# An attention and product-key expert layer: V's gathers ahead of U's, the second keys' one-hot rows of tile 1 on ScalarE, and a different split of the slots at the end

## The reference

```python
q = (h @ w_query).reshape(B, S, PEER_HEADS, 2, PEER_HALF)
s = jnp.einsum('bshcd,hckd->bshck', q, sub_keys)
top_s, top_i = lax.top_k(s, PEER_TOPK)                 # 16 of 128 first keys, 16 of 128 second keys
cand = top_s[..., 0, :, None] + top_s[..., 1, None, :]
best_s, best_i = lax.top_k(cand, PEER_TOPK)            # 16 pairs of them
eid = i1 * N_KEYS + i2                                 # expert = 128 * first key + second key
g = jax.nn.softmax(best_s, axis=-1)
a = jax.nn.gelu(jnp.einsum('td,thkd->thk', hx, expert_u[e]))
out = jnp.einsum('thk,thkd->td', gw * a, expert_v[e])  # 8 heads x 16 experts per token
```

## Time and profile before

| what | value |
|---|---|
| runs, median (lowest to highest) | 1754.23 us (1752.3 to 1754.84) |
| profiled execution: time, span | 1752.67 us, 1750.9 us |
| mean granted TensorE clock | 0.933 of full speed |
| PE, DVE, POOL, ACT busy | 85%, 78%, 55%, 22% of the span |
| DMA, mean | 351 GB/s |
| gathers of U and of V | 256 and 256 |

### The profile page before, as it was taken

How to read it: one execution, slowest core, us unless ns; L and a number is a source line. 1 busy time by engine, 2 the same in 40 slices (tenths; PEclk the granted TensorE clock), 3 DMA queues, 4 the chain that set the end, 5 groups by cost and what they waited for, 6 DMA issues and landing times.

```text
span 1750.9 us, 16867 instructions
## 1 busy us (share of the span) xinstructions
PE 1487.4 (85%) x6164; PEld 931.8 (53%) x6164; DVE 1360.2 (78%) x1915; ACT 380.5 (22%) x822; POOL 967.4 (55%) x591
## 2 busy tenths in 40 slices
...
DMA  9876443466799999999999999999999999999994
GB/s 319 279 262 217 121 145 121 145 203 230 297 380 412 374 424 425 412 425 426 421 424 426 415 425 422 420 426 409 415 427 360 377 414 409 401 404 410 423 428 186
DMA packets 159379, 615.38 MB, mean 351 GB/s; under 512 B 20915, under 2 KB 74255, under 8 KB 96703
## 3 DMA queue, kind: packets, MB, share of 16 engines
q0 software_dynamic: 79232, 485.32, 67.6%
...
HBM read 683.42 MB, written 2.10 MB: 392 GB/s over the span
## 4 chain that ended last, share of the span: by engine, by line
PE 29%; POOL 19%; DMA 19%; DVE 18%; issue 12%; DVEq 2%; ACT 1%; SPq 0%; POOLq 0%; ACTq 0%
DMA v_slot<-in_expert_v_dram,eid 15%; PE psum_all L587 13%; POOL v_slot L542 11%; DVE u_slot L1764 9%; POOL u_slot L525 9%; PE psum_all L727 4%; DVE xh L1799 4%; PE psum_all L976 3%; DMA u_slot<-in_expert_u_dram,eid 2%; PE psum_all L752 2%; PE psum_all L708 1%; PE psum_all L614 1%; PE psum_all L612 1%; PE psum_all L938 1%; DMA wq_ring<-in_w_query_dram 0%
## 5 line engine op out<-in xcount | busy, mean ns | idle before, releaser
L976 PE MATMUL psum_all<-v_slot,diag 128*128 128x512 f32 x1152 | 557.2, 636 | 154.5 <-DMA v_slot<-in_expert_v_dram,eid 108.9
L1764 DVE SCALAR_TENSOR_TENSOR u_slot<-u_slot,xh 128x2048 f32<-128x2048 f32 x256 | 576.2, 2287 | 91.3 <-DMA u_slot<-in_expert_u_dram,eid 90.0
L525 POOL DMA_INDIRECT u_slot<-in_expert_u_dram,eid x256 | 441.7, 1726 | 302.7 <-DVE u_slot L1764 136.7
L542 POOL DMA_INDIRECT v_slot<-in_expert_v_dram,eid x224 | 424.6, 1895 | 94.5 <-issue 64.7
L976 PEld LDWEIGHTS psum_all<-v_slot,diag 128*128 128x128 f32 x1152 | 224.1, 202 | 464.1 <-issue 255.4
L1799 DVE SCALAR_TENSOR_TENSOR xh<-v_slot,gate,xh 128x2048 f32<-128x2048 f32 x112 | 263.4, 2352 | 53.9 <-DMA v_slot<-in_expert_v_dram,eid 46.3
L1382 DVE TENSOR_TENSOR w_lo<-w_ring,w_hi 128x512 fp32r<-128x512 f32 x240 | 156.6, 688 | 78.3 <-ACT w_hi L1012 75.1
L587 PE MATMUL psum_all<-act_hi,w_hi 128*128 128x256 f32 x640 | 185.2, 289 | 1.1 <-DVE w_lo L1382 1.0
L587 PE MATMUL psum_all<-act_hi,w_lo 128*128 128x256 f32 x640 | 181.1, 283 | 0.0
L587 PE MATMUL psum_all<-act_lo,w_hi 128*128 128x256 f32 x640 | 181.0, 283 | 0.0
L1012 ACT ACTIVATE w_hi<-w_ring 128x512 fp32r<-128x512 f32 x240 | 139.4, 622 | 42.7 <-PE psum_all L587 41.5
...
...
## 6 DMA issues: line engine op xcount, KB each, us to landing
...
u_slot<-in_expert_u_dram,eid POOLq DMA_INDIRECT x256, 19.2
v_slot<-in_expert_v_dram,eid POOLq DMA_INDIRECT x256, 18.2
```

The lines of the kernel that those rows point to most:

```text
L525: nc.gpsimd.indirect_dma_start(out=u_slot[m % RU][:, :], out_offset=None, in_=expert_u[0], in_offset=bass.IndirectOffsetOnAxis(ap=eid[:, n ...
L542: nc.gpsimd.indirect_dma_start(out=v_slot[m % RV][:, :], out_offset=None, in_=expert_v[0], in_offset=src, bounds_check=ROWS - 1, oob_is_er ...
L976: ins = nc.tensor.matmul(bank[(4 if n < PH else 0) + q][:, :], diag[:, n % 2, k, :], v_slot[m % RV][:, 512 * q:512 * q + 512], start=(m in ...
L1764: V.scalar_tensor_tensor(u_slot[m % RU][:, :], u_slot[m % RU][:, :], 1.0, xh[:, n // PH, :], ALU.mult, ALU.mult, accum_out=u_dot[:, n, k:k ...
```

## The change

In the gather order GpSimd issues 64 + (m + 1) * 8 / 7 of U's before V's m, so V's run closer behind, and 28 of U's, not 5, are left to be issued in one row before V's gather 144. The ring of dense pieces shrinks from 8 slots to 4 (`RD`) and the distance between the tiles from 3 to 2 (`LEAD`). The four other slots of U join V's ring, from V's gather 151 on (`LATE`), so that V has 11 slots in the last stage. All blocks of tile 1 are built by TensorE behind its last V pick; before they stood between the picks 132 to 143 and behind. For tile 1 ScalarE makes the 128-wide one-hot rows as relu(1 - |iota - key|), eight Abs of 128 columns and one Relu of 1024 per block (`key_rows`); VectorE makes them for tile 0 only. The blocks of tile 0 stand at slightly other places.

```diff
-RD = 8
+RD = 4
-LEAD = 3
+LEAD = 2
+LATE = V0_PICKS + TOPK + RV
+RING_V = list(range(RV, RV + RU - RD)) + [m % RV for m in range(V0_PICKS + TOPK, LATE)]
-HOT0_AT = {180 + 5 * b // 2: b for b in range(NG_T)}
+HOT0_AT = {178 + 2 * b: b for b in range(NG_T)}
...
+    v_slot += u_slot[RD:]
...
-            if m >= PE_PICKS + RV:
-                pool.wait_ge(S["v_dve"], m - RV - PE_PICKS + 1)
+            if LATE <= m < LATE + RU - RD:
+                pool.wait_ge(S["dots_done"], TOPK * NU - RU + v_place(m) - RV + RD + 1)
+            if m >= LATE + RU - RD:
+                pool.wait_ge(S["v_dve"], m - len(RING_V) - PE_PICKS + 1)
...
-            while sent < min(TOPK * NU, TOPK * AHEAD + (m + 1) * 13 // 10):
+            while sent < min(TOPK * NU, TOPK * AHEAD + (m + 1) * 8 // 7):
...
+            if t:
+                pe.wait_ge(S["key_ok"], b + 1)
...
-                pe.wait_ge(S["pick_ok"], 2)
-            if m == V0_PICKS - 2:
-                pick_transposes(1)
-            if m >= V0_PICKS + 4:
-                if m == V0_PICKS + 4:
-                    pe.wait_ge(S["part_ok"], 1)
-                dense_rows(1, m - V0_PICKS - 4)
...
-        for b in range(TOPK - 4, NG_T):
+        pe.wait_ge(S["part_ok"], 1)
+        pick_transposes(1)
+        for b in range(NG_T):
             dense_rows(1, b)
...
+        def key_rows(b):
+            g, n = NG_T + b, PICKS[1]
+            act.wait_ge(S["dense_mm"], g - 1)
+            for i in range(G_TOK):
+                nc.scalar.activation(hot2[0:n, g % 2, i, :], iota_key[0:n, :], ACT.Abs,
+                                     bias=pickT[0:n, 1, 1, G_TOK * b + i:G_TOK * b + i + 1])
+            act.drain()
+            nc.scalar.activation(hot2[0:n, g % 2, :, :], hot2[0:n, g % 2, :, :], ACT.Relu, bias=one_col[0:n, :], scale=-1.0
+                                 ).then_inc(S["key_ok"], 1)
...
+        unit(13)
+        picks_out(1)
+        key_rows(0)
         for b in range(NG_T):
+            if b + 1 < NG_T:
+                key_rows(b + 1)
             if b == 8:
+                expo_gate(14)
+                expo_gate(15)
                 gelu_unit(14)
             dense_out(1, b)
```

More of the change, by code:

```diff
@@ L48, with v_place, v_times @@
 IDS_AT.update({(n, 1): n + 1 for n in range(1, 9)})
-HOT0_AT = {180 + 5 * b // 2: b for b in range(NG_T)}
+HOT0_AT = {178 + 2 * b: b for b in range(NG_T)}
 HOT1_AT = {14 * TOPK + 5 + 3 * b // 2: b for b in range(NG_T)}
+def v_place(m):
+    return m % RV if m < LATE else RING_V[(m - LATE) % len(RING_V)]
+def v_times(m):
+    return sum(1 for i in range(m + 1) if v_place(i) == v_place(m))
 HTW = SEQ + 2
@@ L293, in build @@
     eps = at("eps", [P, 2], F32)
+    one_col = at("one_col", [P, 1], F32)
     warm = at("warm", [P, 1], F32)
@@ L323, in build @@
     s_v = [nc.alloc_semaphore(f"s_v{i}") for i in range(RV)]
+    s_v += [nc.alloc_semaphore(f"s_e{i}") for i in range(RU - RD)]
     s_d = [nc.alloc_semaphore(f"s_d{i}") for i in range(RD)]
@@ L464, in _ @@
         nc.gpsimd.memset(eps[:, 1:2], LN_EPS)
+        nc.gpsimd.memset(one_col[:, :], 1.0)
         nc.gpsimd.memset(cu[:, :, :], 0.0)
@@ L537, in gather_v @@
                 pool.wait_ge(S["v_used"], m - RV + 1)
[L538 to L539 removed]
+            if LATE <= m < LATE + RU - RD:
+                pool.wait_ge(S["dots_done"], TOPK * NU - RU + v_place(m) - RV + RD + 1)
+            if m >= LATE + RU - RD:
+                pool.wait_ge(S["v_dve"], m - len(RING_V) - PE_PICKS + 1)
             src = bass.IndirectOffsetOnAxis(ap=eid[:, n, k:k + 1], axis=0)
             if n < NU - 2:
[L542 to L546 removed]
+                nc.gpsimd.indirect_dma_start(out=v_slot[v_place(m)][:, :], out_offset=None, in_=expert_v[0], in_offset=src,
+                                             bounds_check=ROWS - 1, oob_is_err=False).then_inc(s_v[v_place(m)], 16)
+            else:
+                nc.gpsimd.indirect_dma_start(out=v_slot[v_place(m)][:, :], out_offset=None, in_=expert_v[0], in_offset=src
+                                             ).then_inc(s_v[v_place(m)], 16)
         for m in range(TOPK * AHEAD):
@@ L958, in _ @@
                 pick_transposes(0)
-            if m % 2 and 93 <= m < 93 + 2 * NG_T:
-                dense_rows(0, (m - 93) // 2)
+            if m % 2 and 97 <= m < 97 + 2 * NG_T:
+                dense_rows(0, (m - 97) // 2)
             if m == V0_PICKS:
@@ L1308, in picks_out @@
             n = PICKS[t]
-            nc.scalar.activation(pickT[0:n, t, :, :].rearrange("p a t -> p (a t)"), bank[2 + t][0:n, 0:3 * P], ACT.Copy
-                                 ).then_inc(S["pick_ok"], 1)
+            src = bank[(2, 6)[t]]
+            if t:
+                nc.scalar.activation(pickT[0:n, t, 1, :], src[0:n, P:2 * P], ACT.Copy, scale=-1.0)
+                nc.scalar.activation(pickT[0:n, t, 0, :], src[0:n, 0:P], ACT.Copy)
+                nc.scalar.activation(pickT[0:n, t, 2, :], src[0:n, 2 * P:3 * P], ACT.Copy).then_inc(S["pick_ok"], 1)
+                act.drain()
+            else:
+                nc.scalar.activation(pickT[0:n, t, :, :].rearrange("p a t -> p (a t)"), src[0:n, 0:3 * P], ACT.Copy
+                                     ).then_inc(S["pick_ok"], 1)
+        def key_rows(b):
[4 more added lines that the diff above has]
+                                     bias=pickT[0:n, 1, 1, G_TOK * b + i:G_TOK * b + i + 1])
+            act.drain()
+            nc.scalar.activation(hot2[0:n, g % 2, :, :], hot2[0:n, g % 2, :, :], ACT.Relu, bias=one_col[0:n, :], scale=-1.0
+                                 ).then_inc(S["key_ok"], 1)
         def dense_out(t, b):
@@ L1348, in _ @@
                 diagonals(7)
-            if b in (5, 11):
-                unit(11 + b // 11)
+            if b == 7:
+                unit(11)
             if b == 11:
                 diagonals(8)
+            if b == 15:
+                unit(12)
             dense_out(0, b)
-        unit(13)
-        picks_out(1)
         act.wait_ge(S["t0_part"], 1)
```

19 lines of the change are left out of this document (7 added, 12 removed).

## The result

| | before | changed |
|---|---|---|
| median (lowest to highest) | 1753.26 us (1750.02 to 1754.84, 4 runs) | 1786.4 us (1781.92 to 1792.76, 4 runs) |
| ratio to before | 1 | 1.0193, 95% interval 1.0165 to 1.022 |
| profiled span | 1750.9 us | 1786.5 us |
| mean granted clock of TensorE | 0.933 | 0.927 |

The change costs 33 us. Slower was the likeliest side of the prediction, but 1786 us lies 20 us above its number and 4 us outside its range.

The account below looks back on a forecast made before the run. DMA was taken as full to about 1700 us, with VectorE ending last and 29 us of dense-stage slack. Start 1408 + 307 to tile 0's sum + 47.6 tail gave 1762.6 us of span, so 1766 us; range 1742 to 1782.

Parts of the forecast that it names:

- The gather order up to gather 143: Expert layer: V's gather 143 issued at 1300 us with DMA full; moving tile 0's blocks costs 0, up to 8 us.
- The last 28 of U and the blocks of tile 1: From gather 143 to the dense stage: 4.3 us per block on ScalarE, stage starting at about 1409 us, reckoned as 1408.
- The wait of 14.5 us: VectorE's wait before the first blocks of tile 1, forecast to be gone.
- The dense ring: Dense stage: loads take 8.7 us, so two pieces take 16.1 us against 13.7; tile 0's sum at 1715 us.
- The first rival: Dense ring keeps up, loads landing in under 8.0 us on average; with 7.5 us, time 1746 us; chance 27%.
- V's rows: Dense stage: the slower ring leaves V more of DMA, so VectorE comes to row 246 at about 1687 us.
- The wait and the tail: At row 246, tile 0's statistics, VectorE waits some 28 us for TensorE; then 47.6 us to the end.
- The late blocks: Rival: ScalarE needs 5.3 us per block of tile 1, dense stage starts at 1424 us, time 1782 us; chance 13%.

Follow-up runs that it names:

- a_win95: Changed kernel with TensorE's blocks of tile 0 in front of V picks 95, 97, ... instead of 97, 99, ...: 1815.3 us, ratio 1.0357.
- a_ids: Changed kernel with index work of units 14 and 15 four and six rows sooner, blocks of tile 0 from dot 172 on: 1773.16 us, ratio 1.012.
- a_ids_lead1: Changed kernel with the edits of `a_ids` and LEAD = 1 instead of 2: 1760.61 us, ratio 1.0047.
- b_ring4_lead1: Kernel before with four dense slots instead of eight, the other four in V's ring, and LEAD = 1: 1753.73 us, ratio 1.0013.
- b_ring4: Kernel before with RD = 4, LEAD = 2 and V's ring extended, order and blocks as before: 1770.98 us, ratio 1.0094.

## Why the prediction was wrong

*The gather order up to gather 143: wrong, and this is the step that failed.* Of the blocks' new place the prediction says "a starved queue would cost up to some 8 us, nothing gives a gain. I take 0". DMA lost 17 us there, gather 143 came at 1319.9 us instead of 1300, and the whole chain behind it moved by as much. The argument looked at the queue's 20 us of work and at the two dots by which the blocks moved. It did not ask where each of two engines would now be: at pick 97 TensorE, moved forward by the order, and at dot 178 VectorE, moved back by it. The bound of 8 us came from no row either; by `a_win95` a wait here has no such bound, since GpSimd's one order holds U behind V. `a_ids` takes away the gap and leaves the new order, and has gather 143 at 1297.0 us.

*The last 28 of U and the blocks of tile 1: right in its parts, and the sum right with some luck.* From gather 143 to the dense stage 108 us were forecast and 106 measured, but 115 without the gap (`a_ids`, `a_ids_lead1`). The wait of 14.5 us is gone. ScalarE's blocks follow one another in 3.9 to 4.6 us, two of them in 5.4 and the ninth, with its table loads, in 7.7 us (4.3 were forecast for one without them), and the waits that the profile shows for TensorE before a block all end with VectorE's rows, not with ScalarE, which the prediction had as the slower of the two. ScalarE's Relu takes 1.15 us (1.0). By the page of the Trainium skill that the prediction named (ScalarE: Activation LUTs, What ACT_TABLE_LOAD costs) the estimate was 1.13 us, and here the trace agrees with it.

*The dense ring: right, a little too short.* Two pieces took (1737.29 - 1425.92 - 29.8) / 17 = 16.6 us against 16.1, tile 0's last piece began at +311 instead of +304. Some groups ran at a lower granted clock, 5.40 us instead of 3.60 (0.76 on average from 1728 to 1735 us), and the nine loads issued from 1656.0 us on took 9.0 us in the median. The first rival, a ring that keeps up because loads land in under 8.0 us, is refuted by the 8.7 us of the changed kernel and of `b_ring4_lead1`.

*V's rows: the mechanism right, the size not reached in the changed kernel.* Forecast was VectorE at row 246 at 1687 us, 279 us behind the start of the dense stage. With the ring alone (`b_ring4`) it is there at 1690.5 us, 282 us behind it: the slower ring does leave V more of DMA. In the changed kernel it is 1714.2 us (288 us behind the start) and 1703.3 in `a_ids` (291). The start itself is late by the gap in the first, and in both the new order issues V's gather 144 only some 10 us ahead of the dense stage (1415.6 and 1401.9 us), against 22 us before and in `b_ring4` (1388.0 and 1386.3 us). So VectorE's row 246 is not 16 us sooner than before but 11 us later. The first rival's 1746 us has an error of its own: it keeps the 1687 us, which came from the slow ring, with a ring that keeps up. With such a ring and no gap the statistics start at 1710.2 us and the time is 1760.6.

*The wait and the tail: right, the wait with luck.* It is 24.2 us against 28, since TensorE and VectorE both came to row 246 later than forecast, by 23 and 27 us. The tail has 48.15 us from the statistics to the end against 47.6.

*A reading of before.* The prediction has tile 0's sum there at about 1674 us and 29 us of slack. Behind tile 0's last piece stand four pieces of tile 1 (32 matmuls from 1670.57 us), so the sum was there at 1670.6 us and the slack was 33 us. No term of the forecast hangs on it.

*The late blocks* gave the same number as the upper end of the range, 1782 us, with a start of the dense stage at 1424; it was 1425.9, but not by ScalarE, whose block was as forecast.

In the sum: gather 143 +20, from it to the stage -2, the ring +7, the statistics 2 us closer behind its last piece, the tail +0.5. That is the difference between 1762.6 and 1786.5 us of span. So the number was off by the gap, and the direction was right by the ring, whose cost the prediction had.

Open is how much of the remaining 9 us comes from the order (28 of U's in one row), how much from the blocks that all stand behind the picks, and how much from the smaller moves in ScalarE's order that came with the change; no run undid one of them alone.

## What to carry to other kernels

When an order of transfers is changed, write down for each wait between two engines when each of them arrives, before and after: the order moves one forward and the other back, and the margin shrinks by both. Where DMA is full through a whole stage, count the time that it loses; 19 us of VectorE's work saved, a start 9.5 us earlier and four more slots brought nothing here that could be measured. A ring is judged by the time between a slot's release and its next use against the landing time that the trace shows: one piece less between the two users did as much as four more slots.

## What the runs showed of the chip

- The landing time of a 1 MB load did not depend on how it was spaced: 8.7 us in the median with TensorE waiting for it (the changed kernel), with two rows of time (`b_ring4_lead1`) and with four.
- The granted clock of TensorE was 0.50 (1.2 GHz) from 1330 to 1400 us of `a_ids_lead1`, where it had short blocks between waits, and in the gap of the changed kernel from 1120 to 1140 us, behind a stretch without a matmul; 16 matmuls of a block take 3.63 us there and 1.87 us at 2.4 GHz. From 1410 to 1430 us of `a_ids_lead1`, in the dense stage, it is 1.00 again.
- A wait of one engine came back multiplied in `a_win95`: 9 us more before block 0 made 29 us at the end, over one issue order shared by two rings.
